# All gate tiles of the second branch under the last scan, and the merge tile by tile behind the branch tiles, in a hybrid decoder layer

## The chip, the cores and the metric

One NeuronCore of a Trainium2 chip runs the whole layer. The metric is device microseconds of one execution. TensorE is called PE here (PEld is its weight load), VectorE DVE, ScalarE ACT, GpSimd POOL and SyncE SP.

## What is computed

One layer for 512 tokens of width 1024, in float32. What matters here is the first half of it, between the scan and the output projection:

```
ga, gb, z, xbc, dt = columns of h @ w_in
ya = diff_attention(...)                    # 512 x 1024
yb = ssd_mixer(z, xbc, dt, ...)             # 512 x 2048, 4 groups of 8 heads, chunks of 128 tokens
merged = (jax.nn.sigmoid(ga) * (ya @ w_branch_a[layer])
          + jax.nn.sigmoid(gb) * (yb @ w_branch_b[layer]))
x = x + g1 * (merged @ w_out[layer])
h2 = rmsnorm(x, norm2_g[layer]) * (1.0 + sc2) + sh2
x = x + g2 * moe_ffn(h2, ...)               # 64 experts, top 8, one shared expert
```

## The kernel before

**Matrix products.** Each float32 operand is split into a high and a low part (`hl`, `hT`, `yb_hl`: index 0 and 1 of a pair), and a product is three matmuls, L1376 to L1378. Weights come in units of 128x2048 (1 MB) into a ring of four (`raw`, `hl` over the same place). For each unit ACT copies the high part (L1167, "hi") and DVE subtracts to get the low part (L1697, "lo").

**Order of work.** `plan_steps` writes one list of steps, which PE, ACT, DVE, POOL and SP each walk in the same order, every engine doing its own share of a step. `base` declares a product of some output tiles (128 rows by 512), `out(b, o, ui=...)` places one tile, or, with `ui` 0 or 1, half of its contraction. A tile of a product with width 1024 is 24 matmuls of 512 columns, one of a branch product 12. `item` places a step that is no product. The units of the next product are split behind the first tiles of the one before. SP loads a unit as soon as the one four places ahead in the order of declaration is used up (`half_done`, `proj_done`). Tiles go to two PSUM banks in turn: a tile waits until the one two places ahead has been copied out (`proj_free`). Copies that DVE adds or multiplies go through a buffer of two (`stage`, L1174).

**Around the change.** The branch sums of attention, times sigmoid(ga), are written to DRAM (`gated_a`, "spill") so that `acc` can hold the other branch. Then come four groups g of the state space mixer. In each, z tiles with the convolution; then the scan in the parts "xs" (16 transposes, L1592), 0 to 3 (one chunk each: into the state L1613, heads L1618, decay segments L1565, from the state L1574), "last" and "norm" (16 transposes, L1600); then eight branch tiles (b), which DVE adds to `acc` (L1902). Between the parts of a scan stand tiles that don't depend on it: of the next group, or, in the last group, the first half of gb, whose copy applies the Sigmoid into `gb_sig` (L1244).

Behind the last branch tiles, `item("gate", 0)` multiplies half of `acc` by `gb_sig` (L1911), the second half of gb follows as four tiles that DVE multiplies from `stage` (L1907), and `item("merge", 0)` adds `ga_back` (the spilled half, loaded again by POOL, L1136) in eight operations (L2002). ACT copies the high part (L1346), DVE makes the low part in `hT` (L2005), and only when all eight are there does the output projection ("out") begin:

```
if o == 0:
    if name == "out":
        pe.wait_ge(S["m_lo"], KD)
```

POOL, in the same step, loads `n2b`, `ga_back`, the residual rows `x2` (x in the profile) and prepares constants of the routing. Behind "out" come h2 (norm, router), routing, the shared expert and 64 experts.

## Time and profile before

| | us |
|---|---|
| median of 3 runs | 1880.19 |
| lowest, highest | 1874.66, 1883.25 |
| profiled execution | 1883.58 |
| its span, first to last instruction | 1881.8 |
| PE busy | 1580.4 (84%) |
| DVE busy | 1313.1 (70%) |
| ACT busy | 939.0 (50%) |
| POOL busy | 293.7 (16%) |

The time of an execution is the span and about 1.8 us around it. The span is one long chain that passes through all stages; shares of busy time are averages over them, so a stretch is read by itself. Times in the profile's views are us from the span's start. "PEclk" is the clock that was granted to TensorE as a share of 2.4 GHz. "Idle before" is the time an engine waited ahead of an instruction, with what released it.

### The profile page before, as it was taken

How to read it: one execution, taken by the hardware profiler on the slowest of the kernel's cores; microseconds unless marked ns; L12 is line 12 of the kernel's file. 1: busy time of each engine (PE TensorE's matmuls, PEld its weight loads, DVE VectorE, ACT ScalarE, POOL GpSimd, SP SyncE). 2: the span in 40 equal slices, each digit the busy share in tenths (PEclk: the TensorE clock that was granted, in tenths of full speed). 3: DMA queues.
4: the chain of work that ended last, by engine and by line, in shares of the span. 5: the costliest groups of instructions: out<-in, count | busy, mean ns of one | idle time of the engine just before them, and what ended most of it. 6: DMA issues, size and time to landing. Idle time of an engine off the chain costs nothing.

```text
span 1881.8 us, 22772 instructions
## 1 busy us (share of the span) xinstructions
PE 1580.4 (84%) x7242; PEld 1229.5 (65%) x7243; DVE 1313.1 (70%) x1655; ACT 939.0 (50%) x1146; POOL 293.7 (16%) x282
## 2 busy tenths in 40 slices
PE   6899899998998989988776538999998879999950
PEld 1676676786676776766665437777776668777740
DVE  2786856466857868665556647788887448888849
ACT  2335446433243332433332147788887548888830
POOL 1000000001201002010100542222223112222210
PEclk9899999999999999988887769999999889999985
DMA  8222111445233332212421078899999449999948
GB/s 279 73 71 80 46 49 42 141 145 196 62 98 121 101 112 73 73 45 67 177 68 45 28 290 319 330 372 363 359 373 373 186 184 387 365 354 358 344 178 355
DMA packets 108402, 361.43 MB, mean 192 GB/s; under 512 B 19884, under 2 KB 30320, under 8 KB 81296
## 3 DMA queue, kind: packets, MB, share of 16 engines
q1 hardware_dynamic: 80688, 295.20, 42.8%
q0 software_dynamic: 22688, 45.29, 6.5%
q10 hardware_dynamic: 4928, 19.78, 2.6%
q8 instruction: 44, 0.72, 0.2%
q14 instruction: 54, 0.44, 0.1%
HBM read 352.18 MB, written 43.66 MB: 210 GB/s over the span
## 4 chain that ended last, share of the span: by engine, by line
PE 55%; DVE 16%; DMA 16%; ACT 5%; issue 5%; POOL 2%; SPq 1%; ACTq 0%; POOLq 0%; DVEq 0%
PE psum L1376 15%; PE psum L1378 14%; PE psum L1377 14%; DMA rawm<-in_w_exp_up 10%; DVE cv L1925 2%; PE psum L772 2%; DMA rawm<-in_w_exp_down 2%; POOL slot_table L623 2%; DVE ring L931 2%; PE psum L1409 2%; DVE ofin L1014 2%; ACT ring L859 1%; PE psum L1618 1%; PE psum L1565 1%; ACT hl L1167 1%
## 5 line engine op out<-in xcount | busy, mean ns | idle before, releaser
L931 DVE TENSOR_TENSOR ring<-rawm,ring 128x2048 fp32r<-128x2048 f32 x192 | 436.4, 2286 | 44.6 <-ACT ring L859 44.5
L859 ACT ACTIVATE ring<-rawm 128x2048 fp32r<-128x2048 f32 x192 | 368.1, 1918 | 100.1 <-DMA rawm<-in_w_exp_up 42.4
L1376 PE MATMUL psum<-ring,xT 128*128 128x512 f32 x528 | 224.8, 426 | 29.4 <-DVE ring L931 24.3
L1697 DVE TENSOR_TENSOR hl<-raw,hl 128x2048 fp32r<-128x2048 f32 x59 | 135.0, 2291 | 112.0 <-ACT hl L1167 111.5
L1378 PE MATMUL psum<-ring,xT 128*128 128x512 f32 x528 | 211.2, 400 | 0.0
L1377 PE MATMUL psum<-ring,xT 128*128 128x512 f32 x528 | 210.5, 399 | 0.0
L1376 PE MATMUL psum<-hl,hT 128*128 128x512 f32 x416 | 168.9, 406 | 14.0 <-DVE hT L2005 11.2
L718 POOL DMA_INDIRECT y_rows<-yb,row_of x64 | 98.8, 1544 | 442.4 <-ACT yb L903 433.3
L1377 PE MATMUL psum<-hl,hT 128*128 128x512 f32 x416 | 164.0, 394 | 0.0
L1378 PE MATMUL psum<-hl,hT 128*128 128x512 f32 x416 | 163.8, 394 | 0.0
L1376 PEld LDWEIGHTS psum<-ring,xT 128*128 128x128 f32 x528 | 102.1, 193 | 57.2 <-DVE ring L931 24.5
L1376 PE MATMUL psum<-hT,hl 128*128 128x512 f32 x320 | 134.9, 421 | 0.0
L1377 PE MATMUL psum<-hT,hl 128*128 128x512 f32 x320 | 126.3, 395 | 0.0
L1378 PE MATMUL psum<-hT,hl 128*128 128x512 f32 x320 | 125.9, 394 | 0.0
L1378 PEld LDWEIGHTS psum<-ring,xT 128*128 128x128 f32 x528 | 101.8, 193 | 24.0
L1377 PEld LDWEIGHTS psum<-ring,xT 128*128 128x128 f32 x528 | 102.8, 195 | 18.2
L1174 ACT ACTIVATE stage<-psum 128x512 f32<-128x512 f32 x68 | 40.3, 597 | 147.2 <-PE psum L1378 131.2
L939 DVE TENSOR_TENSOR xT<-psum,xT 128x1024 fp32r<-128x1024 f32 x66 | 80.5, 1220 | 46.5 <-ACT xT L862 44.9
L1167 ACT ACTIVATE hl<-raw 128x2048 fp32r<-128x2048 f32 x59 | 112.5, 1908 | 0.0
L1376 PE MATMUL psum<-ring,aT 128*128 128x512 f32 x264 | 104.8, 397 | 4.4 <-DVE aT L943 4.3
L772 PE MATMUL psum<-ident,xg 128*128 128x128 f32 x512 | 70.2, 282 | 42.9 <-DMA xg<-h_rows,tok_of 28.2
L1377 PE MATMUL psum<-ring,aT 128*128 128x512 f32 x264 | 104.2, 395 | 0.0
(373 smaller groups left out, 3014.6 us busy)
## 6 DMA issues: line engine op xcount, KB each, us to landing
rawm<-in_w_exp_gate SPq DMA_DIRECT2D x64, 1024.0 KB, 12.4
rawm<-in_w_exp_up SPq DMA_DIRECT2D x64, 1024.0 KB, 15.3
rawm<-in_w_exp_down SPq DMA_DIRECT2D x64, 1024.0 KB, 10.1
raw<-in_w_in SPq DMA_DIRECT2D x36, 1024.0 KB, 5.1
modraw<-in_w_ada SPq DMA_DIRECT2D x64, 256.0 KB, 2.9
ysum<-y_rows ACTq DMA_DIRECT2D x16, 1024.0 KB, 9.0
raw<-in_w_ada SPq DMA_DIRECT2D x8, 1024.0 KB, 9.2
raw<-in_w_branch_b SPq DMA_DIRECT2D x8, 1024.0 KB, 5.2
```

Of the source, the lines that this page charges most:

```text
L623: pool.indirect_dma_start(slot_table, bass.IndirectOffsetOnAxis(ap=addr8i[:, t, k:k + 1], axis=0), tokid[:, t, k:k + 1], None).then_inc(S[ ...
L718: pool.indirect_dma_start(y_rows, bass.IndirectOffsetOnAxis(ap=row_of[:, e * NT:e * NT + 1], axis=0), yb[:, e % 2, :], None, bounds_check= ...
L772: ins = tr(xt_dst(k), src[:, k * P:(k + 1) * P], ident[:])
L859: A(ring[:, slot, 1, :], rawm[slot][:], ACT.Copy).then_inc(S["m_hi2"], 1)
L931: TT(ring[:, slot, 0, :], rawm[slot][:], ring[:, slot, 1, :].bitcast(F32), ALU.subtract).then_inc(S["m_lo2"], 1)
L939: return TT(xT[:, par, :, 1, :], psum[:, 0:2].rearrange("p b (k t) -> p (b k) t", t=P), xT[:, par, :, 0, :].bitcast(F32), ALU.subtract)
L1167: A(hl[:, u["n"] % RING, 1, :], raw[u["n"] % RING][:], ACT.Copy).then_inc(S["hi_done"], 1)
L1174: A(stage[:, n % 2], src, func).then_inc(S["proj_free"], 1)
L1376: M(dst, lhs(0), rhs(0), start=first, stop=False)
L1377: M(dst, lhs(0), rhs(1), start=False, stop=False)
L1378: return M(dst, lhs(1), rhs(0), start=False, stop=last)
L1697: TT(hl[:, slot, 0, :], raw[slot][:], hl[:, slot, 1, :].bitcast(F32), ALU.subtract).then_inc(S["lo_done"], 1)
```

## The change

In the last group all eight tiles of gb stand under the scan, in place of four: one ahead of "xs", one each after "xs", 0, 1 and 2, and three over 3, "last" and "norm". Their copies write the plain values into two buffers, `gb_sig[0]` and `gb_sig[1]`, and no longer pass through `stage`. The Sigmoid is applied in place by a step of its own on ACT ("gsig"), one tile ahead of its use. Behind each branch tile k of the last group stands a step "merge" k: DVE multiplies the tile by its gate, adds `ga_back`, and makes the low part of the tile k-1, whose high part ACT has copied. The output projection waits for each tile of the merged input as its contraction comes to it. POOL loads `ga_back` in a step "gload" ahead of the branch tiles, `x2` when four tiles are merged, and does the rest when all are. `gb_sig[1]` lies where the modulation rows had been. The order of declaration puts the weights of gb's second half ahead of the branch weights.

```
@@ -214,6 +214,8 @@
     for g in range(G4):
         z = base("row", ("z", g), halves(w["w_in"], OZ + g * 512), 4)
+        if g == G4 - 1:
+            gb = [base("col", ("gb", h), halves(w["w_in"], OGB + h * 512), 4) for h in range(2)]
         part = lambda p: item("ssd", g, part=p)
...
@@ -221,25 +223,23 @@
             conv(g, *((0,), (1, 2), (3,), ())[o])
             silu(g, *((), (0,), (1, 2), (3,))[o])
-        part("xs")
+        y, x = gb if g == G4 - 1 else (bc(g + 1), xs(g + 1))
         if g < G4 - 1:
-            y, x = bc(g + 1), xs(g + 1)
-            fill = {"xs": [(y, 0)], 0: [(y, 1)], 1: [(x, 0)], 2: [(x, 1)]}
+            fill = {"xs": [(y, 0)], 0: [(y, 1)], 1: [(x, 0)], 2: [(x, 1)], 3: [(x, 2, 0)],
+                    "last": [(x, 2, 1), (x, 3, 0)], "norm": [(x, 3, 1)]}
         else:
-            x = base("col", ("gb", 0), halves(w["w_in"], OGB), 4)
-            fill = {"xs": [(x, 0)], 1: [(x, 1)]}
-        out(*fill["xs"][0])
-        mods(1)
-        for p in (0, 1, 2, 3, "last", "norm"):
+            out(y, 0)
+            fill = {"xs": [(y, 1)], 0: [(y, 2)], 1: [(y, 3)], 2: [(x, 0)], 3: [(x, 1, 0)],
+                    "last": [(x, 1, 1), (x, 2), (x, 3, 0)], "norm": [(x, 3, 1)]}
+        for p in ("xs", 0, 1, 2, 3, "last", "norm"):
             part(p)
-            for f in fill.get(p, ()):
-                out(*f)
-                mods(1)
-            if p in (3, "last"):
-                out(x, 2, ui=(p == "last") * 1)
-            if p in ("last", "norm"):
-                out(x, 3, ui=(p == "norm") * 1)
-                mods(1)
+            for b, o, *ui in fill.get(p, ()):
+                out(b, o, ui=ui[0] if ui else None)
+                if ui != [0]:
+                    mods(1)
+        if g == G4 - 1:
+            item("gload", 0)
+            item("gsig", 0)
         for b in range(2):
...
@@ -250,12 +250,14 @@
                 if g < G4 - 1 and (b, o) in ((0, 3), (1, 1)):
                     silu(g + 1, 4 + b)
+                if g == G4 - 1:
+                    if 4 * b + o < KD - 1:
+                        item("gsig", 4 * b + o + 1)
+                    item("merge", 4 * b + o)
             if b == 0 and g < G4 - 1:
                 mod_rows(6 + 2 * g)
                 mod_rows(7 + 2 * g)
-    item("gate", 0)
-    whole(base("col", ("gb", 1), halves(w["w_in"], OGB + 512), 4))
-    item("merge", 0)
+    item("merge", KD)
     for b in range(2):
...
@@ -421,10 +423,13 @@
     xs_rows = sb("xs_rows", [P, NT, 512])
     lm = sb("lm", [P, 2, GH, P])
+    mod_at = sb.at
     modacc = sb("modacc", [P, 2, T])
     modraw = sb("modraw", [P, 2, T])
     sb.at = xbc_at
-    gb_sig = sb("gb_sig", [P, 4, T])
+    gb_sig = [sb("gb_sig0", [P, 4, T])]
+    sb.at = mod_at
+    gb_sig.append(sb("gb_sig1", [P, 4, T]))
 
...
@@ -1127,16 +1132,18 @@
                     pool.wait_ge(S["stage_used"], spill_at)
                     pool.dma_start(gated_a, acc[:].rearrange("p k t -> p (k t)")).then_inc(S["spilled"], 16)
-                if s["kind"] == "merge":
-
-                    pool.wait_ge(S["proj_done"], out_index[("b", G4 - 1, 1)] + 4)
+                if kind_ == "gload":
+
+                    pool.wait_ge(S["yT_ps"], HEADS + 4 * G4)
                     pool.wait_ge(S["spilled"], 16)
-                    pool.wait_ge(S["stage_used"], USED - 2 * 8 - 3)
                     pool.dma_start(n2b[:], norm2_g.to_broadcast([P, D])).then_inc(S["ga_in"], 16)
                     pool.dma_start(ga_back[:].rearrange("p k t -> p (k t)"), gated_a).then_inc(S["ga_in"], 16)
+                if kind_ == "merge" and s["tag"] == KD:
+                    pool.wait_ge(S["merged"], 4)
                     for t in range(NT):
                         pool.dma_start(x2[:, t, :], x[0, t * P:(t + 1) * P, :]).then_inc(S["x2_in"], 16)
 
+                    pool.wait_ge(S["merged"], KD)
                     pool.dma_start(rbias[:], router_bias.to_broadcast([P, NE])).then_inc(S["rp_in"], 16)
...
@@ -1238,10 +1245,10 @@
                     elif name in ("a", "b", "out", "sdn", "modp"):
                         to_stage(src)
-                    elif name == "ga" or tag == ("gb", 1):
+                    elif name == "ga":
                         to_stage(src, ACT.Sigmoid)
                     elif name == "gb":
-                        free(A(gb_sig[:, o, :], src, ACT.Sigmoid))
+                        free(A(gb_sig[tag[1]][:, o, :], src, ACT.Copy))
                     elif name == "xs":
...
@@ -1340,10 +1347,14 @@
                             a.wait_ge(S["y_ready"], 4 * g + ch - 1)
                             square_sum(ch - 2)
+                elif kind == "gsig":
+                    gate = gb_sig[tag // 4][:, tag % 4, :]
+                    a.wait_ge(S["proj_free"], out_index[("gb", tag // 4)] + tag % 4 + 1)
+                    A(gate, gate, ACT.Sigmoid).then_inc(S["gate_ready"], 1)
                 elif kind == "merge":
-                    for k in range(KD):
-                        a.wait_ge(S["merged"], k + 1)
-                        A(hT[:, k, 0, :], acc[:, k, :], ACT.Copy).then_inc(S["m_hi"], 1)
+                    if tag:
+                        a.wait_ge(S["merged"], tag)
+                        A(hT[:, tag - 1, 0, :], acc[:, tag - 1, :], ACT.Copy).then_inc(S["m_hi"], 1)
                 elif kind == "h2":
...
@@ -1461,9 +1472,7 @@
                     done = b["out0"] + o
                     if o == 0:
-                        if name == "out":
-                            pe.wait_ge(S["m_lo"], KD)
-                        elif name == "sgu":
+                        if name == "sgu":
                             pe.wait_ge(S["h2T_lo"], KD)
...
@@ -1477,6 +1486,8 @@
                         for kk in range(b["ks"]):
                             k = ui * b["ks"] + kk
+                            if o == 0 and name == "out":
+                                pe.wait_ge(S["m_lo"], k + 1)
                             if o == 0 and name in ("a", "b"):
...
@@ -1901,14 +1912,11 @@
                     TT(dst, dst, staged(), ALU.add).then_inc(S["stage_used"], 1)
                     v.wait_ge(S["stage_used"], used[0])
-                elif name == "ga" or tag == ("gb", 1):
+                elif name == "ga":
                     v.wait_ge(S["proj_free"], done)
                     dst = acc[:, tag[1] * 4 + s["o"], :]
                     TT(dst, dst, staged(), ALU.mult).then_inc(S["stage_used"], 1)
                     v.wait_ge(S["stage_used"], used[0])
-                elif kind == "gate":
-                    v.wait_ge(S["proj_free"], out_index[("gb", 0)] + 4)
-                    L(TT(acc[:, 0:4, :], acc[:, 0:4, :], gb_sig[:], ALU.mult))
                 elif kind == "conv":
...
@@ -1995,14 +2003,15 @@
                             y_chunk(ch - 1)
                 elif kind == "merge":
-                    v.wait_ge(S["ga_in"], 32)
-
-                    v.wait_ge(S["proj_done"], out_index[("gb", 1)] + 4)
-                    for k in range(KD):
-                        TT(acc[:, k, :], acc[:, k, :], ga_back[:, k, :], ALU.add).then_inc(S["merged"], 1)
-                    for k in range(KD):
-                        v.wait_ge(S["m_hi"], k + 1)
-                        TT(hT[:, k, 1, :], acc[:, k, :], hT[:, k, 0, :].bitcast(F32), ALU.subtract).then_inc(S["m_lo"], 1)
+                    if tag < KD:
+                        v.wait_ge(S["ga_in"], 32)
+                        v.wait_ge(S["gate_ready"], tag + 1)
+                        L(TT(acc[:, tag, :], acc[:, tag, :], gb_sig[tag // 4][:, tag % 4, :], ALU.mult))
+                        TT(acc[:, tag, :], acc[:, tag, :], ga_back[:, tag, :], ALU.add).then_inc(S["merged"], 1)
+                    if tag:
+                        v.wait_ge(S["m_hi"], tag)
+                        TT(hT[:, tag - 1, 1, :], acc[:, tag - 1, :], hT[:, tag - 1, 0, :].bitcast(F32),
+                           ALU.subtract).then_inc(S["m_lo"], 1)
                 elif name in ("out", "sdn"):
```

On DVE, the second half of the last branch tiles and what stands behind them, before (L1902 accumulates a branch tile, L1697 splits a weight unit, L1911 and L1907 are the gates, L2002 and L2005 the merge):

```order
L1902 TENSOR_TENSOR acc<-acc,stage 128x512 x2
L1911 TENSOR_TENSOR acc<-acc,gb_sig 128x2048
L1907 TENSOR_TENSOR acc<-acc,stage 128x512
L1697 TENSOR_TENSOR hl<-raw_75,hl 128x2048
L1907 TENSOR_TENSOR acc<-acc,stage 128x512
L1697 TENSOR_TENSOR hl<-raw_76,hl 128x2048
L1907 TENSOR_TENSOR acc<-acc,stage 128x512 x2
L2002 TENSOR_TENSOR acc<-acc,ga_back 128x512 x8
L2005 TENSOR_TENSOR hT<-acc,hT 128x512 x8
```

The same place now, from the split behind the first tile to the second tile and, behind the mark, the fifth (L1913 accumulates, L2009 gates, L2010 adds the other branch, L2013 is the low part, L1708 the split):

```order
L1708 TENSOR_TENSOR hl<-raw_78,hl 128x2048
L2009 TENSOR_TENSOR acc<-acc,gb_sig_122 128x512
L2010 TENSOR_TENSOR acc<-acc,ga_back 128x512
L1913 TENSOR_TENSOR acc<-acc,stage 128x512
L2009 TENSOR_TENSOR acc<-acc,gb_sig_122 128x512
L2010 TENSOR_TENSOR acc<-acc,ga_back 128x512
L2013 TENSOR_TENSOR hT<-acc,hT 128x512
...
L1913 TENSOR_TENSOR acc<-acc,stage 128x512
L1708 TENSOR_TENSOR hl<-raw_75,hl 128x2048
L2009 TENSOR_TENSOR acc<-acc,gb_sig_123 128x512
L2010 TENSOR_TENSOR acc<-acc,ga_back 128x512
L2013 TENSOR_TENSOR hT<-acc,hT 128x512
```

Each branch tile is followed by its gate, its addition and the low part of the tile before, where these stood together behind all tiles.

On ACT, the head of the last scan, before (L1261 is the convolution's silu, L1324 copies the transposed xs, L1315 is the exponential of the decay segments, L1244 the gate tile with its Sigmoid, L1167 the high part of a weight unit):

```order
L1261 ACTIVATE cv<-cv 128x512
L1324 ACTIVATE xs_rows<-psum 128x512 x4
L1315 ACT_TABLE_LOAD
L1315 ACTIVATE lm<-psum 128x1024
L1244 ACT_TABLE_LOAD
L1244 ACTIVATE gb_sig<-psum 128x512
L1167 ACTIVATE hl<-raw_75 128x2048
L1315 ACT_TABLE_LOAD
L1315 ACTIVATE lm<-psum 128x1024 x2
L1244 ACT_TABLE_LOAD
L1244 ACTIVATE gb_sig<-psum 128x512
```

The same place now (L1268 is the silu, L1251 the gate tile, L1174 the high part, L1331 the copies of xs, L1322 the exponential):

```order
L1268 ACTIVATE cv<-cv 128x512
L1251 ACTIVATE gb_sig_122<-psum 128x512
L1174 ACTIVATE hl<-raw_75 128x2048
L1331 ACTIVATE xs_rows<-psum 128x512 x4
L1322 ACT_TABLE_LOAD
L1322 ACTIVATE lm<-psum 128x1024
L1251 ACTIVATE gb_sig_122<-psum 128x512
L1174 ACTIVATE hl<-raw_76 128x2048
L1322 ACTIVATE lm<-psum 128x1024
L1251 ACTIVATE gb_sig_122<-psum 128x512
```

A gate tile and a weight split stand ahead of the copies of xs, a second pair behind the first exponential, and the table loads between exponential and gate tile are gone.

## Rows read from the trace of the kernel before

**Rows 1.** Page of the kernel, part 2: two lines of the 40 slices.
```profile
PE   6899899998998989988776538999998879999950
...
PEclk9899999999999999988887769999999889999985
```

**Rows 2.** Busy time by stretch; columns as its first line says.
```profile
core 0: us, PE busy (x) PEld busy (x) DVE busy (x) ACT busy (x) POOL busy (x), PEclk, DMA share, GB/s
806.40:875.00 68.60, 55.69 (x219) 41.55 (x219) 40.58 (x60) 24.43 (x33) 9.99 (x6) 0.83 0.12 41
875.00:897.40 22.40, 22.40 (x97) 18.03 (x96) 11.29 (x10) 10.21 (x11) 0.00 (x0) 1.00 0.29 94
897.40:919.20 21.80, 21.80 (x97) 17.83 (x95) 9.82 (x8) 6.00 (x6) 7.83 (x14) 1.00 0.74 269
919.20:930.60 11.40, 0.19 (x1) 0.00 (x0) 10.41 (x17) 5.44 (x9) 0.00 (x0) 0.68 0.50 191
930.60:937.50 6.90, 6.87 (x24) 5.59 (x25) 0.00 (x0) 0.00 (x0) 0.56 (x1) 0.79 0.13 38
```

**Rows 3.** Timeline, PE, 806 to 875: start, duration, operation, [idle before it].
```profile
809.47 1.09 PE L1592 MATMUL psum<-ident,cv 128*128 128x128 f32 x8 [3.07 <-ACT cv L1261]
...
828.17 2.08 PE L1613 MATMUL psum<-cv,b_rows 128*128 128x512 f32 x2 [4.07 <-DVE cv L1954]
...
851.28 1.78 PE L1574 MATMUL psum<-cv 128*128 128x512 f32 x2 [3.06 <-DVE stage L1941]
...
868.98 3.44 PE L1600 MATMUL psum<-ident,z_rows 128*128 128x128 f32 x16 [2.46 <-DVE z_rows L1976]
```

**Rows 4.** Chain that ended last, 795 to 1110: start, length of the piece.
```profile
830.24 3.31 PE psum L1618 x16
...
843.85 0.86 PE psum L1613 x2
844.71 1.73 PE psum L1618 x16
846.44 1.79 PE psum L1565 x4
...
932.28 0.43 PE psum L1376
```

**Rows 5.** Timeline, ACT, 838 to 938.
```profile
843.03 0.60 ACT L1244 ACTIVATE gb_sig<-psum 128x512 f32<-128x512 f32 x1 [3.60 <-PE psum L1378]
...
864.77 1.28 ACT L1244 ACT_TABLE_LOAD   x1
866.07 0.60 ACT L1244 ACTIVATE gb_sig<-psum 128x512 f32<-128x512 f32 x1
...
878.03 0.60 ACT L1174 ACTIVATE stage<-psum 128x512 f32<-128x512 f32 x1 [2.22 <-PE psum L1378]
...
880.83 0.60 ACT L1174 ACTIVATE stage<-psum 128x512 f32<-128x512 f32 x1 [0.40 <-PE psum L1378]
...
937.72 0.60 ACT L1174 ACTIVATE stage<-psum 128x512 f32<-128x512 f32 x1 [11.30 <-PE psum L1378]
```

**Rows 6.** Timeline, DVE, 860 to 926.
```profile
861.80 0.69 DVE L1943 TENSOR_TENSOR stage<-stage,psum 128x512 f32<-128x512 f32 x1
862.52 0.69 DVE L1946 TENSOR_TENSOR stage<-stage,xs_rows 128x512 f32<-128x512 f32 x1
...
880.54 2.29 DVE L1697 TENSOR_TENSOR hl<-raw,hl 128x2048 fp32r<-128x2048 f32 x1 [1.18 <-ACT hl L1167]
...
920.86 4.90 DVE L2002 TENSOR_TENSOR acc<-acc,ga_back 128x512 f32<-128x512 f32 x8
```

**Rows 7.** DMA issues: KB each, us to landing; last line: the x loads, min/median/max.
```profile
raw<-in_w_in SPq DMA_DIRECT2D x36, 1024.0 KB, 5.1
...
ga_back<-gated_a POOLq DMA_DIRECT2D x1, 2048.0 KB, 9.5
...
DMA to landing us min/median/max: 10.3/11.4/12.5
```

**Rows 8.** Timeline, POOL, 905.
```profile
905.09 0.58 POOL L1135 DMA_DIRECT2D n2b<-in_norm_g  x1 [56.00 <-DVE acc L1907]
```

More of the change, by code:

```diff
@@ L498, in build @@
             "seg_exp", "m_ready", "xd_ready", "ys_ps", "st_ready", "y_ready", "y_read", "yn_ready", "skipped",
-            "g_in", "spilled", "ga_in", "x2_in", "merged", "m_hi", "m_lo")
+            "g_in", "spilled", "ga_in", "x2_in", "merged", "gate_ready", "m_hi", "m_lo")
         sem("h2_row", "h2T_ps", "h2T_hi", "h2T_lo", "h2_out", "wr_in", "lg_ps", "lg_ev",
@@ L517, in stages_out @@
             name = s["tag"][0] if isinstance(s["tag"], tuple) else None
-            return name in ("out", "sdn", "ga", "modp") or s["tag"] == ("gb", 1) or (
+            return name in ("out", "sdn", "ga", "modp") or (
                 s["kind"] == "branch" and s["tag"][1] > 0)
```

## The prediction

> **What bounds the kernel now.** I read first the page's slices. TensorE (PE) is busy in nine tenths or more of nearly every slice, the routing aside, and where it dips around slices 18 to 20 its granted clock dips too [rows 1]: the last scan and the merge lie there. Then a table of that stretch, cut at the points where the work changes [rows 2]. The reader should see two kinds of PE time. In the branch tiles (875.0 to 897.4) and the gate tiles behind them (897.4 to 919.2) PE is busy throughout at a granted clock of 1.00 (2.4 GHz). Then it does nothing for 11.4 us while the merge runs, and starts the output projection at 0.79 on average. In the scan (806.4 to 875.0, 68.6 us) it has 12.9 us without a matmul and a mean clock of 0.83. The timeline of PE names the scan's gaps [rows 3]: 3.07, 4.07, 3.06 and 2.46 us, each behind ACT or DVE, and what follows a gap runs slowly: the 16 small matmuls of L1618 take 3.31 us of the chain behind the second gap and 1.73 us a chunk later, where PE had been busy [rows 4]. So the gaps cost twice. They sum to 12.7 us, and independent matmuls placed there cost little.
>
> **Edit 1: four gate tiles leave the path behind the branches.** The tiles of the second half of gb are 24 matmuls each, 21.8 us together [rows 2], 5.44 us a tile. All of it goes from there, and comes back in edit 4.
>
> **Edit 2: gating and merge per tile.** Before, from the first branch matmul at 875.0 to the copy of the first output tile at 937.7 [rows 5] pass 62.7 us: 22.4 of branches, 21.8 of gate tiles, then the last tile's copy and multiply, 8 additions (4.90 us, [rows 6]) and as many subtractions on DVE, the last handed over at 930.6, and 24 matmuls in 6.9 us. Let T be the first branch matmul. PE gives a branch tile every 2.8 us, the spacing of the copies at 878.03 and 880.83 [rows 5]. DVE now has four operations on each: accumulate, gate, add ga_back, and the low part of the tile before. Dependent operations of 128x512 start 0.72 us apart [rows 6], so a tile takes DVE 2.88 us. A weight split of 2.29 us comes on top in three tiles. DVE therefore takes over as the bound, with a small excess over PE:
> - The first accumulate and the split behind it end at 882.83 in the old run [rows 6], T + 7.8, and they stand in the same places now.
> - The first merge needs ga_back. Its load is now issued after the 16 transposes of L1600, which ended at 872.4, T - 2.6. With 0.58 us for the n2b issue ahead of it [rows 8] and 9.5 us from issue to landing [rows 7] it is there at T + 7.5, just behind the split. I cost it at nothing. The nearest rows are 5.1 us (a w_in unit) and, at worst, 12.5 us (the slowest of the x loads; both [rows 7]), which gives T + 10.5 and 2.7 us lost; two w_out loads fall beside it, so the longer side is the likelier miss.
> - From T + 7.9: 31 operations of 0.72 are 22.3 us (8 gates, 8 additions, 7 accumulates, 8 low parts), and two splits of 2.29 are 4.6 us. That is T + 34.8; 0.7 us for handovers to ACT makes T + 35.5.
> - PE's wait for m_lo is now per k. The products for k = 0 to 6 of the first output tile are done between the subtractions; three remain. At the low clock (0.43 us apart, as behind the 11.2 us gap, [rows 4]) they take 1.3 us. The copy starts near T + 37.0.
>
> PE gets pauses at the end of this stretch, so the low clock goes on into the second output tile; that first tile lost 6.9 - 5.4 = 1.5 us to it before [rows 2], and I take 1.0 us. So 62.7 becomes 38.0: **a gain of 24.7 us**. The floor is DVE's own work from its first copy (T + 3.6): 32 times 0.72 and three splits are 29.9 us, hence T + 33.5 and a copy at T + 35. The ceiling is in the rivals.
>
> **Edit 3: ACT and the queues.** ACT used to change its table at each gate tile: six table loads in this stretch of the program, now two, so 4 x 1.28 us go. They lay in idle time (behind the load at 838.15 ACT still waited 3.60 us for PE, [rows 5]), so I cost them at nothing. The Sigmoids now run one tile ahead, 0.6 us each. With copy and high part a tile needs 1.8 us of ACT against 2.88 of DVE: hidden. One table load remains ahead of the first branch copy. The load at 864.77 and its Sigmoid at 866.07 start 1.30 us apart [rows 5], so load and Sigmoid (1.9 us) fit in the 2.22 us that ACT waited before the copy at 878.03. Beside it: the Trainium skill, ScalarE: Activation LUTs, "What ACT_TABLE_LOAD costs", puts a change of table at about 2.66 us with the drain. By that the first copy would come 1.0 us late, and the sum would be a gain of 23.7 in place of 24.7. I keep the row.
>
> POOL issues the same DMAs and operations in the same order with other waits. The x loads wait for the fourth merged tile: T + 7.9 + 13 x 0.72 = T + 17.3, about 2 us for four issues, the slowest landing 12.5 us later, T + 32. DVE wants them behind the copy at T + 37. What is queued behind them (rbias, the table's first fill) waits for the eighth tile, near T + 34, and is read only in routing, about 80 us later: hidden. On SP the two gate units are loaded before the two branch units. The gate units wait for the z tiles (806 at the latest) and land in about 5.1 us [rows 7], before the second gate tile needs its half. The first w_out units wait for the last gate tile, land about T + 5, and are split only in the fifth and sixth branch tile: cost nothing.
>
> **Edit 4: the scan takes four more blocks.** Gate tiles now stand ahead of "xs", after "xs", 0, 1, 2, split over 3 and "last", and three in all between "last" and "norm" where there was one. PE's own work at full clock bounds this from below: 8 tiles of 5.44 are 43.5 us, seven matmuls with the state or into it at 0.86 are 6.0, four groups of L1618 at 1.73 are 6.9, three of L1565 at 1.79 are 5.4 [rows 4], and 32 transposes are 4.4 if 8 take 1.09 [rows 3]. The sum is 66.2 us, less than the 68.6 of now, because the gaps' slow clock goes as well. What stays idle: the tile ahead of "xs" puts a split of 1.91 us on ACT and 2.29 on DVE before the copies of xs and the chunk inputs, which I follow to a first chunk 2.6 us later than now; the second split likewise, of which the full clock wins most back. Before the last transposes PE now has 10.9 us of tiles (5.4 before) for a DVE and ACT chain of 8 us, so it comes late by 3 us, and runs the transposes at full clock. I take 4.4 us idle: 70.6 us, **a loss of 2.0 us**. The ends: -2.4 us, and +30.2, of which the slower rival below speaks.
>
> **Sum.** 24.7 - 2.0 = 22.7 us. Everything behind the first output tile hangs on it in a chain through h2, routing and the experts, whose first loads wait for the last shared tile, so the gain should reach the end whole. The profiled execution took 1883.6 us (span 1881.8 and 1.8 around it) and would take 1860.9. The median of the three runs is 3.4 us lower: **1857.5 us**. A difference under 0.5%, 9.4 us, is about what runs of this kernel (1874.7 to 1883.3) can't tell from none.
>
> **Rivals.**
> - *Half of the blocks find no cover.* The scan is a chain of PE, ACT and DVE steps, and a block of 5.44 us is longer than any gap. If two of four count in full, the scan grows by 11 us: gain 13.7, 1866.5 us. For it: the extra splits. Against: L1618 nearly halves in time when PE has been busy.
> - *TensorE stays at 1.2 GHz.* Gaps of 2.5 to 4 us left the scan at a mean of 0.83, and behind the one of 11.2 us matmuls came 0.43 us apart in place of 0.23. In the new branch stretch DVE paces PE, with a pause per tile. If PE ran it at the low clock, 96 and 24 matmuls at 0.427 us take 51.2 us and outlast DVE: 62.7 becomes 51.5, net gain 9.2, 1871.0 us. Against: the pauses are mostly 1 us or less, the gaps that cost the clock were 2.5 and more. Beside it: the Trainium skill, TensorE: Matmul & The Clock Gate, "HAM oscillation", describes bursts of matmuls split by waits that run cold every time. It speaks against this change, and by it this rival's sum holds.
> - *Slower: the scan's chain takes every block.* Its place is the scan between 806 and 875. If the ACT and DVE steps start only after each block and the clock doesn't recover, four blocks cost 21.8 us, and the two splits that moved in cost 2 x (1.91 + 2.29) = 8.4 us, while the stretch behind gains 24.7: 5.5 us slower, 1885.7. It decides as soon as the scan grows by more than 24.7 us. Against it: the blocks are independent of the scan, and the gaps exist.
> - *The change moves work but frees nothing*, because DVE's merge work is on the path in both orders: then only the four tiles' move counts and the total is within a few us of now. Against: PE waited 11.4 us with 9.8 us of DVE work that now lies under the branches.
>
> **How the numbers follow.** Forecast 0.70, 1851 to 1864 us. Half the blocks uncovered 0.16. Low clock 0.07. Slower 0.04. Frees nothing 0.03. Faster by over 0.5%: 0.70 + 0.16 and a sliver of the low clock's, 0.87; within 0.5%: 0.09; slower: 0.04. The range: the best scan (-2.4 in place of +2.0) and the floor of edit 2 (2 us more) give 1851, and a margin of 1 us for the runs 1850; upwards it takes in the uncovered blocks and reaches the low clock, 1871.
>
> **What would show it.** The ga_back additions start about 8 us after the first branch matmul and lie 3 to 5 us apart; the gap of 11.2 us before the first output matmul is gone, and small gaps stand between its triples; the first output copy comes 37 us after the first branch matmul and about 22 us earlier than 937.7; the scan lasts 69 to 73 us with the clock near 1. A scan above 80 us, a first ga_back addition later than T + 11, or a clock near 0.6 in the branch tiles would make the prediction wrong; so would a stretch from the first output tile to the end that is longer than before.

## The result and the profile after

| | before | after |
|---|---|---|
| median, first comparison | 1881.72 us (4 runs) | 1858.9 us (4 runs, 1854.0 to 1863.5) |
| ratio, 95% interval | | 0.9883 (0.9842 to 0.9925) |
| median, second comparison | 1881.46 us (13 runs) | 1855.9 us (4 runs, 1849.3 to 1864.5) |
| ratio, 95% interval | | 0.9842 (0.9815 to 0.9869) |
| span of the profiled execution | 1881.8 us | 1852.3 us |

The change saves 22.8 us in the one comparison and 25.6 us in the other; 22.7 was forecast. Both differ from no change by more than the 0.5% of the prediction.

The stretches of the changed kernel, cut where the work changes, answer to [rows 2] and have its columns:

```profile
803.60:871.80 68.20, 65.93 (x316) 51.32 (x315) 44.56 (x63) 23.47 (x34) 11.12 (x8) 1.00 0.20 72
871.80:894.40 22.60, 21.85 (x94) 17.30 (x93) 15.79 (x20) 16.48 (x22) 2.08 (x4) 1.00 0.70 251
894.40:908.70 14.30, 9.05 (x30) 5.97 (x29) 11.78 (x16) 4.01 (x7) 2.74 (x9) 0.83 0.45 162
908.70:915.10 6.40, 6.40 (x25) 5.18 (x25) 3.68 (x3) 2.40 (x2) 0.40 (x1) 0.85 0.19 59
```

The first line is the scan: PE lacks a matmul for 2.3 us of 68.2, and its clock is 1.00, where it was 12.9 of 68.6 and 0.83. The second and third are the branches and the first output tile, with the pauses at their end. The 0.83 of the third line is a mean of two levels: windows cut finer give 1.00 until 903.1 and 0.50, that is 1.2 GHz, from 904.2 to 910.5. The fourth is the next output tile, 6.4 us in place of 5.44.

All waits of PE from the last z tile to the first output tile, for [rows 3]. A timeline line gives start, duration, operation and, in brackets, the idle time before it with what ended it:

```profile
812.07 1.15 PE L1603 MATMUL psum<-ident,cv 128*128 128x128 f32 x8 [2.10 <-ACT xs_rows L1331]
855.43 1.10 PE L1585 MATMUL psum<-cv 128*128 128x512 f32 x2 [0.17 <-DVE stage L1949]
...
883.91 0.50 PE L1387 MATMUL psum<-yb_hl,hl 128*128 128x512 f32 x1 [0.75 <-ACT stage L1181]
...
896.13 0.50 PE L1387 MATMUL psum<-hl,hT 128*128 128x512 f32 x1 [0.75 <-ACT stage L1181]
900.54 0.47 PE L1387 MATMUL psum<-hl,hT 128*128 128x512 f32 x1 [1.37 <-DVE hT L2013]
903.10 0.50 PE L1387 MATMUL psum<-hl,hT 128*128 128x512 f32 x1 [1.63 <-DVE hT L2013]
905.75 0.80 PE L1387 MATMUL psum<-hl,hT 128*128 128x512 f32 x1 [1.50 <-DVE hT L2013]
```

Of the four gaps of the scan one of 2.10 us is left, and the 11.23 us at the merge have become three waits of about 1.5 us between groups of three matmuls of the first output tile, and two of 0.75 us for a PSUM bank. The timeline of DVE (same columns) shows who sets the pace there: the first gate, one ordinary tile (accumulate, gate, addition, low part), and the end.

```profile
881.29 0.69 DVE L2009 TENSOR_TENSOR acc<-acc,gb_sig 128x512 f32<-128x512 f32 x1 [1.69 <-DMA ga_back<-gated_a]
...
885.28 0.68 DVE L1913 TENSOR_TENSOR acc<-acc,stage 128x512 f32<-128x512 f32 x1
886.00 0.69 DVE L2009 TENSOR_TENSOR acc<-acc,gb_sig 128x512 f32<-128x512 f32 x1
886.72 0.69 DVE L2010 TENSOR_TENSOR acc<-acc,ga_back 128x512 f32<-128x512 f32 x1
887.33 0.68 DVE L2013 TENSOR_TENSOR hT<-acc,hT 128x512 fp32r<-128x512 f32 x1
...
905.01 1.47 DVE L2013 TENSOR_TENSOR hT<-acc,hT 128x512 fp32r<-128x512 f32 x2
```

From 881.29 to 906.48 DVE doesn't pause. The view of the tile ga_back gives the landing of the load that it waited for first, 11.2 us after the issue at 870.07, and the timeline of ACT the first branch copy and the copy of the first output tile:

```profile
DMA to landing us min/median/max: 11.2/11.2/11.2
```

```profile
872.60 1.28 ACT L1353 ACT_TABLE_LOAD   x1
873.89 0.63 ACT L1353 ACTIVATE gb_sig<-gb_sig 128x512 f32<-128x512 f32 x1
874.80 0.60 ACT L1181 ACTIVATE stage<-psum 128x512 f32<-128x512 f32 x1 [0.27 <-PE psum L1389]
...
908.72 0.60 ACT L1181 ACTIVATE stage<-psum 128x512 f32<-128x512 f32 x1 [2.96 <-PE psum L1389]
```

Two lengths carry the rest of this text. **S** runs from the end of the last z matmul to the first branch matmul, **B** from there to the copy of the first output tile.

| kernel | S | B | median, ratio to before (95%) |
|---|---|---|---|
| before | 68.6 | 62.7 | |
| after | 68.1 | 36.9 | 1858.9, 0.9883 (0.9842 to 0.9925) |
| after_again | 68.1 | 35.9 | 1855.9, 0.9842 (0.9815 to 0.9869) |
| tiles_only | 68.1 | 48.2 | 1864.5, 0.9909 (0.9884 to 0.9934) |
| merge_only | 68.6 | 55.3 | 1874.5, 0.9966 (0.9946 to 0.9986) |
| short_gates | 56.3 | 36.5 | 1839.0 (one run), see below |
| spread4 | 57.6 | 63.2 | 1874.9, 0.9953 (0.9934 to 0.9973) |
| lead_all | 69.8 | 36.8 | 1861.1, 0.9882 (0.9848 to 0.9915) |
| no_ga_add | 68.2 | 30.6 | 1840.5 (one run), see below |
| ga_first | 68.1 | 35.2 | 1855.7 (one run) |
| pool_add | 68.2 | 37.8 | 1857.3, 0.9861 (0.9838 to 0.9885) |
| sig_in_copy | 69.4 | 37.2 | 1858.0, 0.9873 (0.9848 to 0.9899) |

S + B falls from 131.3 to 105.0, less 1.0 of slow clock in the next tile: 25.3 us. The profiled span fell by 29.5. The other 4.2 us lie outside: the z tiles end at 803.6 and not 806.4, and what follows the second output copy is 1.5 us shorter. Neither can be put down to the change. In eleven profiles of kernels with the same code up to there (lead_all's is other) the z tiles end anywhere from 803.6 to 811.2. And what follows the first output copy, 943.6 us after the change and 944.1 before it, takes from 937.2 to 947.5 us in the ten profiles of kernels that leave no arithmetic out. So a total of one run says little, and S and B are the measure in what follows.

short_gates and no_ga_add leave out part of the arithmetic, and what follows their first output copy takes 935.3 and 931.9 us, shorter than in any other profile. A good part of their low totals comes from there, and why wasn't looked into; only their S and B are used.

### The profile page after: what moved, and what is told of

Its sections match the earlier page's. It is cut to its first block, busy times and chain, and to the rows that moved or that the text cites. A ratio compares the mean times of both kernels' runs of the same rounds, so it can differ in the third digit from the quotient of the medians.

```text
span 1852.3 us, 22775 instructions
## 1 busy us (share of the span) xinstructions
PE 1566.3 (85%) x7242; PEld 1220.1 (66%) x7243; DVE 1312.3 (71%) x1658; ACT 936.8 (51%) x1150; POOL 292.4 (16%) x282
## 4 chain that ended last, share of the span: by engine, by line
PE 55%; DMA 17%; DVE 16%; issue 5%; ACT 5%; POOL 2%; SPq 1%; ACTq 0%; POOLq 0%; DVEq 0%
PE psum L1387 14%; PE psum L1389 14%; PE psum L1388 14%; DMA rawm<-in_w_exp_up 10%; PE psum L777 2%; DMA rawm<-in_w_exp_down 2%; POOL slot_table L628 2%; DVE ring L936 2%; PE psum L1420 2%; DVE ofin L1019 2%; DVE cv L1933 2%; ACT ring L864 1%; PE psum L1576 1%; PE psum L1629 1%; ACT hl L1174 1%
## 5 line engine op out<-in xcount | busy, mean ns | idle before, releaser
L1708 DVE TENSOR_TENSOR hl<-raw,hl 128x2048 fp32r<-128x2048 f32 x59 | 135.0, 2291 | 113.1 <-ACT hl L1174 112.5
L1174 ACT ACTIVATE hl<-raw 128x2048 fp32r<-128x2048 f32 x59 | 112.4, 1907 | 0.3 <-DMA raw<-in_w_in 0.3
L1387 PE MATMUL psum<-ring,aT 128*128 128x512 f32 x264 | 105.4, 399 | 4.2 <-DVE aT L948 4.1
L1389 PE MATMUL psum<-ring,aT 128*128 128x512 f32 x264 | 104.9, 398 | 0.0
L1388 PE MATMUL psum<-ring,aT 128*128 128x512 f32 x264 | 104.8, 397 | 0.0
```

The source lines that it names most:

```text
L1174: A(hl[:, u["n"] % RING, 1, :], raw[u["n"] % RING][:], ACT.Copy).then_inc(S["hi_done"], 1)
L1387: M(dst, lhs(0), rhs(0), start=first, stop=False)
L1388: M(dst, lhs(0), rhs(1), start=False, stop=False)
L1389: return M(dst, lhs(1), rhs(0), start=False, stop=last)
L1708: TT(hl[:, slot, 0, :], raw[slot][:], hl[:, slot, 1, :].bitcast(F32), ALU.subtract).then_inc(S["lo_done"], 1)
```

## The experiments

### One part of the change alone

**tiles_only.** The merge steps stand in one block behind the branches.

```
-                    item("merge", 4 * b + o)
...
-    item("merge", KD)
+    for k in range(KD + 1):
+        item("merge", k)
...
-                                pe.wait_ge(S["m_lo"], k + 1)
+                                pe.wait_ge(S["m_lo"], KD)
```

> All eight gate tiles stay under the scan; gating, addition and low parts stand in one block behind the eighth branch tile, and the output projection waits for all of it, as before the change. Two lengths are compared, S: end of the last z matmul to the first branch matmul (68.6 us before the change, 68.1 after it), and B: first branch matmul to the copy of the first output tile (62.7 and 36.9). My theory, that the tiles are covered by waits in the scan and that the merge is a second and separate saving: S stays 67 to 70, B is 22.4 of branches, 0.6 and 0.7 for the last copy and sum, 8 times 2.0 on DVE, 0.7, and 6.9 of slow matmuls: 47 to 48. So 15 to 16 us faster than before the change, 10 slower than after. Rival, that the saving needs both parts because the gap at the merge only moves: B near 37 or total within 4 us of the changed kernel. Rival, that the scan was freed by something else: S above 72.

S is 68.1, B 48.2, and the time 17.0 us under the kernel before. PE waits 17.32 us for the last low part:

```profile
916.35 0.77 PE L1386 MATMUL psum<-hl,hT 128*128 128x512 f32 x1 [17.32 <-DVE hT L2012]
```

This is the better part of the gain alone: 17.0 us in the total and 15.0 in S + B, where 15 to 16 was expected.

**merge_only.** The planner's order of before, with four gate tiles behind the branches, and the merge steps spread. The high and low parts must wait for the last gate tile, since gate tiles read hT and these parts overwrite it.

```
+                if g == G4 - 1 and b == 0:
+                    ...
+                    item("merge", o)
...
+    x = base("col", ("gb", 1), halves(w["w_in"], OGB + 512), 4)
+    for o in range(4):
+        out(x, o)
+        item("gsig", 4 + o)
+        item("merge", 4 + o)
+    item("merge", KD)
```

> The gate tiles stay where they were before the change, four under the scan and four behind the branches. Tiles 0 to 3 are gated and merged behind their branch tiles, 4 to 7 behind their gate tiles, high and low parts follow behind the last gate tile (which still reads hT), and the output projection waits per tile. My theory: S 68 to 69 as before the change. B is 22.4 + 21.8, a gap of 2.5 to 3.5 us (copy, Sigmoid, high part, low part) in place of 11.2, and 5.4 to 6.5 of matmuls: 53 to 54. So 8 to 10 us faster than before; with the other part alone (15 to 16) this makes about the whole 25 that the traces show. Rival, that the wait at the merge is worth its 11.2 us only with the tiles moved: B above 58, under 5 us faster.

B is 55.3, and PE's wait for the first low part is 3.57 us in place of 11.23:

```profile
925.48 0.50 PE L1391 MATMUL psum<-hl,hT 128*128 128x512 f32 x1 [3.57 <-DVE hT L2017]
```

S + B falls by 7.4 us, the time by 7.0 us. That is less than the 8 to 10 expected: behind the wait of 3.57 us the first output tile ran in part at the low clock and took 7.35 us to its copy, where 5.4 to 6.5 was taken. B is still below the rival's 58. The two parts give 15.0 and 7.4 us in S + B, 22.4 together, of the 25.3 and 26.0 that the whole gives in its two profiles (less the slow clock of the next tile): they are separate savings. The rest of about 3 us came only with both parts. A likely reason, not tested by itself, is that low parts can be made between branch tiles only when no gate tile reads hT any more.

**after_again.** No edit.

> The changed kernel once more, on the chip of the two others. The stretches repeat: S 68, B 37, 1.0 us of slow clock in the next output tile. 20 to 28 us faster than before the change. The scan's beginning, which came 2.7 us earlier in the profile of the changed kernel although nothing ahead of it changed, should come back within a few us either way; if it is earlier again by 2.7, something ahead of the scan did change.

S 68.1 and B 35.9 repeat. The z tiles end at 811.16, 7.5 us later than in the first profile: what lies ahead of the last scan varies by itself. The scans of groups 0 to 2, whose order the change leaves as it was, take from 65.2 to 68.7 us in the eleven profiles with the same code. Their waits agree (but for the first of group 0, 4.97 to 6.06 us); what differs is the granted clock. It is 0.95 to 0.97 in the scans of up to 67.1 us and 0.92 to 0.93 in those of 67.6 and more. The same wait of 2.52 us ahead of the last transposes of group 1 is followed by 16 transposes in 1.97 us in the first profile of the changed kernel and in 3.60 us in this one (first and second line):

```profile
631.75 1.97 PE L1611 MATMUL psum<-ident,z_rows 128*128 128x128 f32 x16 [2.52 <-DVE z_rows L1984]
...
637.84 3.60 PE L1611 MATMUL psum<-ident,z_rows 128*128 128x128 f32 x16 [2.52 <-DVE z_rows L1984]
```

So a wait of this length is followed by the low clock in one execution and not in the next, and a difference of up to 3 us in the length of a scan with waits can be the clock's alone.

### What the scan is bound by

**short_gates.** Half the contraction of the gate tiles is left out.

```
+                            if name == "gb" and kk not in (0, b["ks"] - 1):
+                                continue
```

> Leaves out half of the contraction of the eight gate tiles: 12 matmuls in each in place of 24, so 21.8 us less PE work in the scan; all else as in the changed kernel. My theory, that the scan is a chain of PE, ACT and DVE steps whose waits the tiles fill: S falls by 5 to 9 us only, to 59 to 63, the gaps come back (about 3 us each) and with them a mean clock near 0.85. Rival, that the scan is now bound by PE throughout: S falls by about 20, to 48, with the clock still near 1. B stays at 36 to 38 in both.

S is 56.3: of the 21.8 us that were taken from PE, 11.8 came back. Neither number was right. The waits did come back, 8.6 us in all, but with a short tile in every place the longest is 1.9 us, and the clock stayed at 0.97, not 0.85:

```profile
809.20:865.50 56.30, 47.66 (x219) 34.11 (x218) 44.94 (x63) 23.47 (x34) 10.94 (x8) 0.97 0.26 88
```

So with 96 gate matmuls, spread, the scan is bound by its chain at some 57 us. (How long it is without any wasn't run.) The changed kernel has 66 us of PE work in it and is bound by PE, and its 192 gate matmuls cost 12 us more than 96 do. But the kernel before also had 96 in its scan, in five places, and took 68.6 us. The next run puts that to the test.

**spread4.** The kernel before, its four gate tiles as eight halves.

```
+            halfs = {"xs": (0, 1), 0: (1, 0), 1: (1, 1), 2: (2, 0), 3: (2, 1), "last": (3, 0), "norm": (3, 1)}
+            out(x, 0, ui=0)
+            for p in ("xs", 0, 1, 2, 3, "last", "norm"):
+                part(p)
+                out(x, halfs[p][0], ui=halfs[p][1])
```

> The kernel before the change, with one edit: its four gate tiles under the last scan (96 matmuls, the same work as in short_gates) are cut into eight halves, one in each place between the parts, the first ahead of xs. The other four stay behind the branches. What short_gates suggests (S fell to 56.4 us with 96 gate matmuls in eight places, where the kernel before takes 68.6 with 96 in fewer places): the place of the tiles matters more than their number, since every gap left open costs its length and the slow clock behind it. Then S is 56 to 59, B stays 62.7, and the kernel is 10 to 12 us faster than before without any tile moved off the path. Rival, that short_gates was fast for another reason (no table loads, shorter blocks ahead of the last transposes): S above 64.

S is 57.6 and B stays at 63.2; the time is 8.7 us lower. With the same matmuls the clock of this stretch is 0.94, where [rows 2] have 0.83: it is 1.00 up to 852.5, where the one long wait begins, and 0.50 for about 5 us behind that.

```profile
806.90:864.50 57.60, 48.12 (x219) 34.81 (x218) 40.59 (x60) 24.31 (x33) 9.95 (x6) 0.94 0.14 49
```

That wait, of 5.17 us, is the one ahead of the last transposes; the others are 1.3 us or less. Cutting the tiles and placing them evenly was alone worth 11 us, and the change spent it at once on four more tiles.

**lead_all.** A tile ahead of xs in the groups 0 to 2 too, the others one place up.

```
+        out(y, 0)
         if g < G4 - 1:
-            fill = {"xs": [(y, 0)], 0: [(y, 1)], 1: [(x, 0)], 2: [(x, 1)], 3: [(x, 2, 0)],
-                    "last": [(x, 2, 1), (x, 3, 0)], "norm": [(x, 3, 1)]}
+            mods(1)
+            fill = {"xs": [(y, 1)], 0: [(x, 0)], 1: [(x, 1)], 2: [(x, 2, 0)], 3: [(x, 2, 1)],
+                    "last": [(x, 3, 0)], "norm": [(x, 3, 1)]}
```

> The changed kernel, and in the groups 0 to 2 too a tile stands ahead of xs; the six tiles of a group are moved one place up, so that the places behind 2 and last have half a tile less. The wait of 4.97 us ahead of xs in each of these groups should go, and the slow transposes and tile behind it (3.8 us for 16 transposes where PE had been busy 2.2; 6.9 for a tile in place of 5.5). If waits and clock decide there as in the last group: 2 to 4 us less in each, 6 to 11 in all, faster than the changed kernel (1845 to 1851 where that has 1857). Rival: DVE paces these groups (53.3 us busy of 68.3, with the modulation slices), and what is gained ahead of xs is waited for behind 2 and last: within 3 us of the changed kernel.

Not faster (1861.1 against 1855.9 to 1858.9): the scans of the groups take 68.0, 68.2 and 68.5 us. For group 2 that is slower, since it takes 65.5 to 65.8 in all the other profiles. The wait of 4.97 us ahead of xs is gone but for 2.10 us within it, and the one ahead of the last transposes has grown from 2.80 to 5.22 us, as the rival said. That DVE paces these groups, the rival's reason, isn't shown by it. In group 2:

```profile
701.35 1.66 PE L1604 MATMUL psum<-ident,cv 128*128 128x128 f32 x8 [2.10 <-ACT xs_rows L1332]
...
754.23 3.67 PE L1612 MATMUL psum<-ident,z_rows 128*128 128x128 f32 x16 [5.22 <-DVE z_rows L1985]
```

The last scan, whose order this run leaves alone, is 1.6 us longer than in the changed kernel (69.8), with the same waits. Here the clock fell to 0.50 for about 3 us behind the wait of 2.10 us, which it didn't in the changed kernel (8 transposes in 1.58 us, there in 1.15):

```profile
820.63 1.58 PE L1604 MATMUL psum<-ident,cv 128*128 128x128 f32 x8 [2.10 <-ACT xs_rows L1332]
```

**sig_in_copy.** The Sigmoid in the copy of the gate tiles, as before the change.

```
-                        free(A(gb_sig[tag[1]][:, o, :], src, ACT.Copy))
+                        free(A(gb_sig[tag[1]][:, o, :], src, ACT.Sigmoid))
```

> The changed kernel with the Sigmoid applied in the copy of the gate tiles, as before the change; the steps on ACT that apply it later are gone, eight operations fewer. The table loads in this stretch of the program rise from two to nine. The prediction put the table loads at nothing. If that holds, S stays 68 to 69 (a load ahead of an exponential starts while ACT waits for PE anyway), B is the same or up to 1 us shorter, and the time is within 2 us of the changed kernel. Rival: with a tile in every place ACT has less idle time, each load of 1.28 us (two per chunk) or the drain around it falls into the chain from the segments to the chunk's heads: S 72 to 78.

Seven more table loads cost 1.3 us in S (69.4, just above what was expected) and nothing that the total shows. Most of them start while ACT has nothing else to do: behind the first load below ACT still waited 3.32 us for PE before the exponential. The one at 853.41 started only when that wait was over. The gate copy behind it began 1.3 us later for it, and PE's wait for the steps that follow, 0.17 us in the changed kernel, is 1.46 us: this one load accounts for the whole 1.3 us.

```profile
832.64 1.28 ACT L1322 ACT_TABLE_LOAD   x1
837.24 1.03 ACT L1322 ACTIVATE lm<-psum 128x1024 f32<-128x1024 f32 x1 [3.32 <-PE psum L1574]
...
853.41 1.28 ACT L1251 ACT_TABLE_LOAD   x1 [3.86 <-PE psum L1387]
```

B was expected the same or up to 1 us shorter and is 37.2, longer by 0.3 to 1.3 us. ga_back landed 11.5 us after its issue here, 11.2 and 10.2 in the two profiles of the changed kernel.

### What the branch stretch is bound by

**no_ga_add.** The additions of ga_back are left out; its load and the wait for it stay.

```
-                        TT(acc[:, tag, :], acc[:, tag, :], ga_back[:, tag, :], ALU.add).then_inc(S["merged"], 1)
```

> Leaves out the eight additions of ga_back; its load and the wait for it stay. If DVE bounds the stretch behind the scan, B falls by most of 8 times 0.6 to 0.7 us until PE bounds it (22.6 of branches, 5.4 of the first output tile, about 4 from the last branch tile to its low part): 36.9 becomes 31.5 to 33. If B is set by the landing of ga_back and the turn of the PSUM banks, it stays above 35.5.

B is 30.6, a little below what was expected, though ga_back landed as late as 11.4 us after its issue, and PE is busy in 29.05 us of it:

```profile
876.20:906.80 30.60, 29.05 (x122) 22.40 (x121) 22.05 (x27) 20.41 (x30) 3.75 (x10) 1.00 0.72 261
```

DVE's operations set B in the changed kernel, and PE is the next bound, 5 to 6 us below.

**ga_first.** The load of n2b moves behind the fourth merged tile.

> The load of n2b no longer stands ahead of that of ga_back, but behind the fourth merged tile. ga_back landed at T + 9.5 (11.2 us after its issue), and DVE waited 1.7 us for it. Theory: the issue is 0.6 us earlier and half a megabyte less is in flight with it, so it lands 0.6 to 1.7 us earlier and B falls by as much, to 35.2 to 36.3. Rival, that the two w_out units in flight set the landing: 0.6 at most.

ga_back lands 8.4 us after its issue, where it took 10.2 to 11.5 in the six profiles with n2b ahead of it and all eight gate tiles, in full, under the scan. B is 35.2, 0.8 below after_again and 1.8 below the first profile. The two profiles of the changed kernel agree with that: landing after 11.2 and 10.2 us goes with a B of 36.9 and 35.9. The next tile loses 0.2 us to the clock in place of 1.0, because here the clock fell and came back some 3 us earlier in the stretch; that this is the load's doing isn't shown. The total of one run (1855.7) can't tell.

**pool_add.** GpSimd adds ga_back, the parts follow two tiles behind.

```
+                    nc.gpsimd.tensor_tensor(acc[:, k, :], acc[:, k, :], ga_back[:, k, :], ALU.add).then_inc(
+                        S["merged"], 1)
```

> The changed kernel with the eight additions of ga_back on GpSimd, the load of ga_back ahead of that of n2b (ga_first), and high and low parts two tiles behind, not one, to leave GpSimd time. no_ga_add showed what lies in the eight additions: without them B fell from 36 to 30.6. If GpSimd does one in 1.1 to 2 us, inside the 2.8 us that PE needs for a branch tile, B falls to 31 to 33, and the kernel is 3 to 5 us faster than the changed one. Rival: DVE operations that run beside GpSimd's take up to three times as long (2.39 us for one of 0.69 beside a GpSimd operation in the scan), which eats it: B 36 to 40, same time or slower. The last tile also has a longer way through GpSimd, about 1 us in either case.

The rival holds: B 37.8, and 1857.3 us is the changed kernel's time. One GpSimd addition takes 1.60 to 1.68 us, inside the 1.1 to 2 us that the theory wanted, but each makes one DVE operation that starts beside it last 1.67 to 1.78 us in place of 0.69. The 1.0 to 1.1 us that DVE loses there is more than the 0.6 to 0.7 us that the addition had taken of it. The timeline of POOL has two of them, that of DVE what ran meanwhile:

```profile
886.40 1.67 POOL L1147 TENSOR_TENSOR acc<-acc,ga_back 128x512 f32<-128x512 f32 x1 [0.64 <-DVE acc L2016]
...
888.70 1.67 POOL L1147 TENSOR_TENSOR acc<-acc,ga_back 128x512 f32<-128x512 f32 x1 [0.63 <-DVE acc L2016]
```

```profile
886.95 1.67 DVE L2016 TENSOR_TENSOR acc<-acc,gb_sig 128x512 f32<-128x512 f32 x1
...
889.14 1.77 DVE L1921 TENSOR_TENSOR acc<-acc,stage 128x512 f32<-128x512 f32 x1
```

## Why the prediction was right, step by step

**The sum** (22.7 us; measured 22.8 and 25.6, and 25.3 within the two stretches of the first pair of profiles). The mechanism is the forecast one: tiles_only and merge_only separate its two parts. That the first comparison comes within 0.1 us of the sum is chance: in the stretches the sum was 2.6 us short, nearly all of it in the scan, and the four runs behind the median differ by 9.5 us.

**Edit 2, B of 37.0 us:** 36.9 and 35.9. Three of its terms were off and cancel. The first gate came at T + 9.5 and not T + 7.9, because ga_back took 11.2 us to land; the prediction named this as the likelier miss. From there to the last low part DVE needed 25.2 us, where the sum had 27.6 (22.3, 4.6 and 0.7): only operations that use the result just ahead of them start 0.72 us apart, the others 0.6, so a tile takes 2.65 us and not 2.88. From the last low part to the copy it took 2.2 us, where the sum had 1.5: six matmuls were left at the low clock, not three, since PE's last wait, up to 905.75, stood ahead of the products of k = 6. The handovers to ACT cost almost nothing. The slow clock behind the first output tile was 1.0 us, as taken (1.3 in after_again).

**Edit 4, S of 70.6:** 68.1 to 68.2, in the changed kernel and four of its variants (69.4 and 69.8 in two others, explained above). S was to grow by 2.0 us and fell by 0.5. The bound of 66.2 us of PE work holds (65.9 us busy), but 2.3 us are idle where 4.4 were taken. The reason given for the scan's cover was right as a sum and incomplete as an explanation. It said that the gaps cost twice and that blocks placed there cost little. spread4 and short_gates show that the four additional tiles aren't free: they cost 10 to 12 us against a scan of 57, and the even placing of the tiles gives 11 us back through waits and clock. The two came out equal, which the sum had from PE's work (66.2 us against the 68.6 of before). The prediction also says that three tiles stand between "last" and "norm"; there are two, and its 10.9 us are those of two. Read as a rule that tiles under a scan are free, the prediction would have been wrong.

**Edit 3.** Table loads at nothing: sig_in_copy finds 1.3 us in S for seven of them, from the one that no wait covered. The first branch copy came 3.0 us after the first branch matmul, with a table load and a Sigmoid ahead of it, and 3.0 before the change without them. The 2.66 us that the Trainium skill gives for a change of table (ScalarE: Activation LUTs, "What ACT_TABLE_LOAD costs") would have made it 1.0 us later; load and Sigmoid started 1.29 us apart. The measurement decides for the row. The loads of x, issued at 890.37, landed in 3.7 to 6.0 us, far ahead of their use at 909.

**The rivals.** Half of the blocks uncovered, and all of them (slower): S didn't grow, so neither came as a time. The first one's mechanism is there, though. It had two of four blocks count in full, 11 us, and against spread4 and short_gates the four tiles cost 10.5 to 11.8 us. The low clock: the branch stretch ran at 1.00 throughout, and so did the first output tile until about 903.7. There PE was in the second of two bursts of three matmuls, which had waits of 1.4 and 1.6 us ahead of them, and from there to 910.5 the clock was 0.50. Of the bursts that run cold every time, which the Trainium skill describes (TensorE: Matmul & The Clock Gate, "HAM oscillation"), this case shows one such stretch at the very end, where PE isn't the bound, and 1.0 us of loss behind it. Merge work that frees nothing: PE's wait of 11.2 us went, and tiles_only shows it at 17.3 when the merge is put back as a block.

**The signs.** The first ga_back addition started at T + 10.2, not T + 8 and short of the T + 11 that would have spoken against the prediction, and the additions lie 2.1 to 4.9 us apart, not 3 to 5. The scan lasted 68.1 us, just under the 69 to 73. The copy of the first output tile came 36.9 us after the first branch matmul, as said, and 29 us earlier than 937.7, of which 2.8 lie ahead of the scan.

What stays open: why the clock falls behind a wait in one execution and not in another. The four runs of after_again have spans of 1847.5, 1853.7, 1854.6 and 1862.7 us and mean clocks of 0.938, 0.936, 0.934 and 0.931, so much of what differs between runs may be this; that it also accounts for the 7.5 us ahead of the last scan wasn't followed up. The next gain is also only pointed to: no_ga_add says that 5 to 6 us lie in DVE's operations behind the scan, but nothing tried took them off DVE at a profit.

## What to carry to other kernels

When independent matmuls fill the waits of a dependent chain, their placing counts as much as their number: one in every gap keeps each wait short and the clock up, and 96 matmuls in eight places took 11 us less than in five. Before adding more, sum PE's work in the stretch against the chain's own length. The two amounts that were run (48 us of work in a scan of 57, and 66 in one of 68) fit the rule that a tile costs little up to the chain's length and its full time beyond it; nothing between them was run. And a block that stands between two products is best done tile by tile behind the first of them, with the second waiting per tile; the bound is then the elementwise engine's operations per tile, and its first input must have landed by then.

## What the runs showed of the hardware that wasn't expected

A DVE operation of 128x512 that started beside a GpSimd addition of the same shape (1.67 us) took 1.67 to 1.78 us in place of 0.69 in pool_add and ended some 0.55 us after it (888.62 and 888.07), so that moving work from a full DVE to an idle GpSimd gained nothing. With half a megabyte issued ahead of it on the same queue, the load of 2 MB landed 10.2 to 11.5 us after its issue in six profiles; with that half megabyte much later or right behind it, 8.4 us (ga_first) and 9.4 us (pool_add), one profile each. The order isn't all of it: merge_only and short_gates have 9.6 and 9.7 with the half megabyte ahead. And PE's granted clock isn't settled by the length of a wait: waits of 1.4 and 1.6 us with a burst of 0.9 us between them ended at 0.50, the same wait of 2.10 us was followed by 1.00 in the changed kernel and by 0.50 in lead_all, and one of 2.52 us likewise in two executions of the changed kernel.
